# A decoder trunk on one core: the weight ring laid flat, its slots 8 and 16 bytes around the activation buffers' offset modulo 256

## What is computed

```python
for i in range(DEPTH):                                   # DEPTH = 2, x is (1, 256, 2048) f32
    xn = rmsnorm(h, g_mix[i])
    mix = attn_mixer(xn, ...) if i % 2 == 0 else rglru_mixer(xn, ...)   # xn @ w_in, ... @ w_out
    h = h + mix
    h = h + swiglu(rmsnorm(h, g_ffn[i]), w_ffn_gate[i], w_ffn_up[i], w_ffn_down[i])
    gate = sigmoid(rmsnorm(h, g_ple[i]) @ w_ple_gate[i])
    h = h + gate * (p[i] @ w_ple_proj[i])
return rmsnorm(h, g_final)
```

## Time and profile before

| | |
|---|---|
| median of 3 runs | 2473.3 us (2473.11 to 2473.95) |
| profiled execution | 2473.23 us |
| its span, first to last instruction | 2471.5 us |
| TensorE matmul busy | 2445.6 us (99%), 11084 instructions |
| TensorE weight load busy | 1994.7 us (81%) |
| DVE busy | 1315.4 us (53%) |
| ACT busy | 1139.5 us (46%) |
| mean DMA rate | 180 GB/s |
| granted TensorE clock, mean | 0.997 |

### The profile page before, as it was taken

The page is one execution under the profiler, slowest core; times in us unless marked ns, Lnnn a source line. Parts: engine busy times, 40 slices in busy tenths (PEclk is TensorE's granted clock), DMA queues, the critical chain, the costliest instruction groups (busy, mean ns, idle before and its releaser), DMA issues.

```text
span 2471.5 us, 29756 instructions
## 1 busy us (share of the span) xinstructions
PE 2445.6 (99%) x11084; PEld 1994.7 (81%) x11084; DVE 1315.4 (53%) x1677; ACT 1139.5 (46%) x1533; POOL 3.2 (0%) x17
## 2 busy tenths in 40 slices
PE   8999999999999999999999999999999999999997
PEld 7888778888888888888888888888888888888886
DVE  5545665555454454444566676554454454444455
ACT  5435555544444444444454575544444444344454
POOL 0000000000000000000000000000000000000000
PEclk9999999999999999999999999999999999999999
DMA  7744435666666665555557445566666666555563
GB/s 215 229 120 120 131 117 182 185 187 186 187 187 182 186 186 184 187 188 187 187 187 235 140 154 178 186 183 185 187 187 184 186 183 188 186 187 187 187 204 135
DMA packets 234042, 443.87 MB, mean 180 GB/s; under 512 B 16184, under 2 KB 21344, under 8 KB 233824
## 3 DMA queue, kind: packets, MB, share of 16 engines
q1 hardware_dynamic: 233904, 442.62, 58.7%
q10 hardware_dynamic: 48, 0.02, 0.0%
HBM read 440.49 MB, written 2.10 MB: 179 GB/s over the span
## 4 chain that ended last, share of the span: by engine, by line
PE 96%; DVE 1%; ACT 1%; DMA 1%; issue 0%; ACTq 0%; DVEq 0%
PE ps L1278 30%; PE ps L1276 30%; PE ps L1277 30%; PE ps L1232 2%; PE ps L1487 1%; PE ps L1400 1%; PE ps L1331 1%; DMA raw<-in_w_in_rec_dram 1%; DVE w_lo L774 0%; ACT w_hi L537 0%; PE ps L1412 0%; PE ps L1437 0%; ACT prob L691 0%; DMA h<-in_x_dram 0%; PE ps L1371 0%
## 5 line engine op out<-in xcount | busy, mean ns | idle before, releaser
L774 DVE TENSOR_TENSOR w_lo<-raw,w_hi 128x1024 fp32r<-128x1024 f32 x820 | 998.4, 1220 | 1071.1 <-ACT w_hi L537 1070.1
L537 ACT ACTIVATE w_hi<-raw 128x1024 fp32r<-128x1024 f32 x820 | 863.1, 1055 | 1137.3 <-PE ps L1278 1108.2
L1278 PE MATMUL ps<-w_hi,xa_lo 128*128 128x512 f32 x1664 | 656.9, 395 | 0.0
L1277 PE MATMUL ps<-w_lo,xa_hi 128*128 128x512 f32 x1664 | 654.2, 393 | 0.0
L1276 PE MATMUL ps<-w_hi,xa_hi 128*128 128x512 f32 x1664 | 653.9, 393 | 0.0
L1277 PEld LDWEIGHTS ps<-w_lo,xa_hi 128*128 128x128 f32 x1664 | 312.7, 188 | 73.1
L1276 PEld LDWEIGHTS ps<-w_hi,xa_hi 128*128 128x128 f32 x1664 | 312.6, 188 | 70.5
L1278 PEld LDWEIGHTS ps<-w_hi,xa_lo 128*128 128x128 f32 x1664 | 312.6, 188 | 68.8
L1276 PE MATMUL ps<-w_hi,xb_hi 128*128 128x512 f32 x864 | 351.3, 407 | 3.9 <-DVE xb_lo L837 2.3
L1278 PE MATMUL ps<-w_hi,xb_lo 128*128 128x512 f32 x864 | 341.9, 396 | 0.0
L1277 PE MATMUL ps<-w_lo,xb_hi 128*128 128x512 f32 x864 | 341.0, 395 | 0.0
(11 more groups left out here) (200 smaller groups left out, 1043.9 us busy)
## 6 DMA issues: line engine op xcount, KB each, us to landing
raw<-in_w_ffn_gate_dram SPq DMA_DIRECT2D x176, 512.0 KB, 3.6
raw<-in_w_ffn_up_dram SPq DMA_DIRECT2D x176, 512.0 KB, 3.6
raw<-in_w_ffn_down_dram SPq DMA_DIRECT2D x176, 512.0 KB, 3.6
raw<-in_w_in_attn_dram SPq DMA_DIRECT2D x88, 512.0 KB, 3.7
raw<-in_w_ple_gate_dram SPq DMA_DIRECT2D x64, 512.0 KB, 3.8
raw<-in_w_in_rec_dram SPq DMA_DIRECT2D x64, 512.0 KB, 4.3
raw<-in_w_out_attn_dram SPq DMA_DIRECT2D x32, 512.0 KB, 3.7
raw<-in_w_out_rec_dram SPq DMA_DIRECT2D x32, 512.0 KB, 3.7
```

Source lines behind the costliest of these rows:

```text
L537: nc.scalar.activation(w_hi[:, s, 0:n], raw[:, s, 0:n], ACT.Copy).then_inc(hi_ready, 1)
L774: nc.vector.tensor_tensor(w_lo[:, s, 0:n], raw[:, s, 0:n], w_hi[:, s, 0:n].bitcast(F32), ALU.subtract).then_inc(lo_ready, 1)
L1277: nc.tensor.matmul(o, xh[:, k, tok], w_lo[:, s, wk], start=False, stop=False)
L1278: ins = nc.tensor.matmul(o, xl[:, k, tok], w_hi[:, s, wk], start=False, stop=(k == nkt - 1))
```

## The change

The ring of `w_hi` and of `w_lo` becomes one flat row of elements. Place s begins at element `W_AT[s]`: 1024 s + 4, 6, 10 or 12. Both tensors are put at an address that is 224 modulo 256, and `a_off` is rounded up to a multiple of 256. So places 0 to 3 begin 240, 248, 8 and 16 bytes above a multiple of 256, and with activation buffers at 0 that is d = -16, -8, +8 and +16 for places 0, 1, 2 and 3. Places 0 and 3 begin at multiples of 16 bytes, places 1 and 2 only at multiples of 8; none begins at a multiple of 64. The elements inside a place follow each other as they did. The addresses of the small tensors between `w_lo` and `a_off` move as well (from 128 to 32 modulo 256 for `stage`, `pT_hi` and `ident`; `h` stays at 128), and the buffers behind `a_off` move with it from 192 to 0. With `pT_hi` and `pT_lo` at 32, the eight slots of `w_ple_proj` get d = -48, -40, -24 and -16 in places 0 to 3. No instruction is added, removed or put elsewhere, on any engine or queue; shapes, waits and the order are the same. In the changed kernel's listing the lines move by two: L537 becomes L539, L774 becomes L776, and the matmuls L1278 to L1280.

```diff
--- before.py
+++ after.py
@@ -58,7 +58,7 @@
 LRU_C = 8.0
 NBLK = 8
 XPAD = 260
-WROW = 2 * CW + 32
+W_AT = tuple(CW * 2 * s + c for s, c in enumerate((4, 6, 10, 12)))
 
 
 class Kind:
@@ -251,8 +251,10 @@
 
         h = put("h", [NT, D])
         raw = put("raw", [NRING, 2 * CW])
-        w_hi = put("w_hi", [NRING, WROW], F32R)
-        w_lo = put("w_lo", [NRING, WROW], F32R)
+        top[0] += (224 - top[0]) % 256
+        w_hi = put("w_hi", [W_AT[-1] + 2 * CW + 4], F32R)
+        top[0] += (224 - top[0]) % 256
+        w_lo = put("w_lo", [W_AT[-1] + 2 * CW + 4], F32R)
         stage = put("stage", [NT, CW])
         sg = put("sg", [NT, CW])
         junk = put("junk", [CW], BF16)
@@ -277,7 +279,7 @@
         ssqb = put("ssqb", [NT, HEADS])
         rstdb = put("rstdb", [NT, HEADS])
         sp_t = put("sp_t", [6, KD])
-        a_off = top[0]
+        a_off = (top[0] + 255) // 256 * 256
         big = a_off + 2 * KD * S * 4
         s_off = big + 2 * KD * S * 4
         assert big + 2 * KF * S * 4 <= base + size - 64, (big + 2 * KF * S * 4, base + size)
@@ -534,7 +536,7 @@
                 act.wait_ge(raw_in[s], dma_no(t, s))
                 if not (isinstance(t, int) and t < NRING):
                     act.wait_ge(w_used, t - (NRING - 1))
-                nc.scalar.activation(w_hi[:, s, 0:n], raw[:, s, 0:n], ACT.Copy).then_inc(hi_ready, 1)
+                nc.scalar.activation(w_hi[:, W_AT[s]:W_AT[s] + n], raw[:, s, 0:n], ACT.Copy).then_inc(hi_ready, 1)
 
             def evacuate(q, i, r):
 
@@ -771,7 +773,7 @@
                 _, nk, _, w = slot_shape(q, r, j)
                 n = nk * w
                 dve.wait_ge(hi_ready, t + 1)
-                nc.vector.tensor_tensor(w_lo[:, s, 0:n], raw[:, s, 0:n], w_hi[:, s, 0:n].bitcast(F32),
+                nc.vector.tensor_tensor(w_lo[:, W_AT[s]:W_AT[s] + n], raw[:, s, 0:n], w_hi[:, W_AT[s]:W_AT[s] + n].bitcast(F32),
                                         ALU.subtract).then_inc(lo_ready, 1)
 
             def evacuate(q, i, r):
@@ -1262,20 +1264,20 @@
 
                     o = ps[0:NGATE, 2 * r, 0:S]
                     for k in range(k0, k0 + nk):
-                        wk = slice((k - k0) * w, (k - k0 + 1) * w)
-                        nc.tensor.matmul(o, w_hi[:, s, wk], xh[:, k], start=(k == 0), stop=False)
-                        nc.tensor.matmul(o, w_lo[:, s, wk], xh[:, k], start=False, stop=False)
-                        ins = nc.tensor.matmul(o, w_hi[:, s, wk], xl[:, k], start=False, stop=(k == nkt - 1))
+                        wk = slice(W_AT[s] + (k - k0) * w, W_AT[s] + (k - k0 + 1) * w)
+                        nc.tensor.matmul(o, w_hi[:, wk], xh[:, k], start=(k == 0), stop=False)
+                        nc.tensor.matmul(o, w_lo[:, wk], xh[:, k], start=False, stop=False)
+                        ins = nc.tensor.matmul(o, w_hi[:, wk], xl[:, k], start=False, stop=(k == nkt - 1))
                     ins.then_inc(w_used, 1)
                     return
                 for m in range(NT):
                     o = ps[:, EX + m if ple_p else 2 * r + m, c0:c0 + w]
                     for k in range(k0, k0 + nk):
                         tok = slice(m * P, (m + 1) * P)
-                        wk = slice((k - k0) * w, (k - k0 + 1) * w)
-                        nc.tensor.matmul(o, xh[:, k, tok], w_hi[:, s, wk], start=(k == 0), stop=False)
-                        nc.tensor.matmul(o, xh[:, k, tok], w_lo[:, s, wk], start=False, stop=False)
-                        ins = nc.tensor.matmul(o, xl[:, k, tok], w_hi[:, s, wk], start=False,
+                        wk = slice(W_AT[s] + (k - k0) * w, W_AT[s] + (k - k0 + 1) * w)
+                        nc.tensor.matmul(o, xh[:, k, tok], w_hi[:, wk], start=(k == 0), stop=False)
+                        nc.tensor.matmul(o, xh[:, k, tok], w_lo[:, wk], start=False, stop=False)
+                        ins = nc.tensor.matmul(o, xl[:, k, tok], w_hi[:, wk], start=False,
                                                stop=(k == nkt - 1))
                 ins.then_inc(w_used, 1)
```

## The result

| | before | changed |
|---|---|---|
| median | 2473.52 us (4 runs, 2473.11 to 2473.95) | 2492.86 us (4 runs, 2492.81 to 2492.99) |
| ratio | | 1.0078, 95% interval 1.0061 to 1.0096 |
| span of the profiled execution | 2471.5 us | 2491.1 us |

The changed kernel is slower, by 19.3 us or 0.8%. The forecast was 2443 us.

The account below looks back on a forecast made before the run. TensorE bounds the kernel, by the distance between matmul starts. Ring offsets gain 40 us, less 8 for jumps and 1.5 for offsets, about 30; the rest nothing: 2473 us becomes 2443 us, range 2435 to 2500.

Parts of the forecast that it names:

- the floor: Full-width weight matmuls: 226.7 ns between starts taken as the least possible, with loads costing nothing at d = 0.
- Steps 2 to 6: `w_ple_proj` slots, `gates` slots, small tensors, ACT's and DVE's writes, and order, waits and DMAs: no change in time from any.
- step 1: The ring's new offsets in 808 slots: matmuls near 226.7 ns, gain 30 us, at most 40 us.
- The other term of step 1: Slots' first matmuls after a jump of d: 0.01 us lost a slot, 8 us over 808 slots.
- Only one side of zero is good: Rival on the ring: places 0 and 1 at 233.3 ns, 2 and 3 at 226.7, about 2472 us; chance 0.18.
- its variant: In the ring, places 1 and 2, only at multiples of 8 bytes, are the slow ones; same time, about 2472 us.
- An offset off 64 bytes costs every place a step: Rival on the ring: 33 pieces of 64 bytes instead of 32, 233.3 ns everywhere, 24 us more, 2497 us; chance 0.22.
- The pace doesn't follow d: Rival on the weight matmuls: something other than d sets their distance, time stays at 2473 us; chance 0.10.
- the second rival: The rival of a step for every offset off 64 bytes, in all ring places: 2490 to 2500 us, chance 0.22.

Follow-up runs that it names:

- e4_shift32: The changed kernel with weights and activation buffers both 32 bytes further on, d still -16, -8, +8, +16: 2493.00 us.
- e5_zero32: The changed kernel with d = 0 in all four places and both operands 32 bytes further on: 2435.12 us, ratio 0.9857 to before.
- e1_zero: The changed kernel with all four places at d = 0, both operands at multiples of 256: 2433.74 us, ratio 0.9846 to before.
- e9_minus16: The changed kernel with d = -16 in all four places: 52.6 us above the kernel before.
- e2_quarters: The changed kernel with places 0 to 3 at d = 0, 64, 128, 192: 2472.70 us.
- e3_lines: The changed kernel with places 0 to 3 at d = 0, 16, 32, 48: 2480.18 us.
- e8_plus16: The changed kernel with d = +16 in all four places: 6.9 us above the kernel before.

## Why the prediction was wrong

**What held.** TensorE bounds the kernel, and the distance between matmul starts decides its time. That distance goes with d, the moving operand's start less the stationary one's modulo 256, and not with the address or the place: e4_shift32 and e5_zero32 show it directly. 226.7 ns is what d = 0 gives, and e1_zero turns it into time. Two readings behind this were off and changed nothing. `pT_hi` lay 64 bytes off the activation buffers, not 128; the values of d given for it are right. And the `gates` slots of the earlier trace rows, my support for the floor, weren't at d = 0 (+64 and -32 there), and the 113.3 ns are from the fastest of them: the three slots before the last take 1.40, 1.38 and 1.37 us. From e1_zero to e9_minus16 the same instructions take 90 us more. The Trainium skill's rule of two independent read ports ("TensorE: Matmul & The Clock Gate", section "Step-by-step: what each phase is for"), by which the time would have stayed, isn't borne out for this stream. Steps 2 to 6 held: writes at multiples of 8 bytes cost nothing (1221 and 1056 ns), the distances behind all other matmuls add up to 165.1 us against 165.9, and the weight loads waited 2.8 us for DVE where it was 3.9.

**What failed is one sentence of step 1**: "being four to eight times nearer to 0, I take 226.7 to 227.0". I interpolated between points 64 bytes apart as if the pace were smooth in d. It isn't. With one offset throughout, +16, -8, +8 and -16 cost 6.9, 13.5, 20.8 and 52.6 us more than the kernel before, where d = 0 gives 37.5 less. Eight bytes to either side of the best point the launch takes longer than with 64 bytes to both sides by turns. The text had the warning itself, "No row shows an offset that isn't a multiple of 64", and the 1.5 us that I put on this gap had no row behind it: the next known values on either side lay 1.6 and 6.6 ns above, which on 9696 matmuls is 16 and 64 us, and the steepest of these offsets went beyond both (10 ns at d = -16).

**The other term of step 1**, what a slot loses when d jumps, was taken at 8 us. The 0.02 us a slot was right for a slot that has d = 0 (e2_quarters; 0.05 us in e3_lines), and e1_zero, without jumps, got the whole 40 us less 2.5. In the changed kernel the term has nothing to act on, since no place has a fast pattern to return to.

**The rivals.** "Only one side of zero is good" falls: neither side is. So does its variant, that only the places at multiples of 8 bytes are slow: all four are, and with one offset throughout -16 is the slowest. "An offset off 64 bytes costs every place a step" had the sign and nearly the time (2497 us), but its mechanism, a further piece of 64 bytes at every start off such a multiple, is refuted by e5_zero32. That its time came so near is luck: 233.3 ns is near what most values of d give, as 128 and 192 did in the kernel before. "The pace doesn't follow d" falls with e1_zero. The range, 2435 to 2500, held the result, because it had been drawn to reach the second rival.

## What to carry to other kernels

Where TensorE is the bound and streams float32r, 512 columns at a time, against a load of 128 columns that runs beside it (no other shape or type was tried at full load), put the moving and the stationary operand at the same offset modulo 256, exactly and in every buffer and ring place, by rounding their bases up and keeping pitches at multiples of 256; here that is 1.5% of the launch for a few lines. A pad that seems harmless (32 elements on a ring's row) is enough to lose it. And before forecasting from a curve, ask at which spacing its points were taken: across a gap the bound is at least the worst value known, not the nearest one, and here even the worst one known was passed.

## What the runs showed of the hardware that I had not expected

- The good point is narrower than 8 bytes on either side (one run each at 8 bytes): 2433.7 us at d = 0, but 2485.0 at -8 and 2492.3 at +8.
- The pace isn't a function of d alone. At d = -16 slots run at 226.7, 233.3 or 236.7 ns, and slot 819, with the same addresses in both, runs at 236.7 in the changed kernel and at 226.7 in e8_plus16. At d = 0 in all places nearly all slots have the fast one in e1_zero: in 765 of 808 the last six distances are 226.5 to 227.5 ns, and in the other 43, all but two of them among the first 93 slots, 228.3 to 232.5.
- Narrowing two of three products to 32 stationary columns made the stream slower, 27.9 us over the launch at d = 0, with the order of the products turned as well.
